# One weight sum in four, of each seven-product gate/up step, made by a negated ScalarE copy and an accumulating DMA

## The reference

```python
def swiglu(h, w_gate, w_up, w_down):
    return (jax.nn.silu(h @ w_gate) * (h @ w_up)) @ w_down

for i in range(DEPTH):                       # DEPTH = 2
    ...                                      # token mixer
    h = rmsnorm(x, g[2])
    x = x + rmsnorm(swiglu(h, ffn_w_gate[i], ffn_w_up[i], ffn_w_down[i]), g[3])
```

## Time and profile before

| | us |
|---|---|
| median of 3 runs | 1317.84 (1317.77 to 1318.12) |
| profiled execution, its own time | 1318.55 |
| its span, first to last instruction | 1316.7 |
| TensorE busy | 1305.5 (99%) |
| VectorE busy | 991.8 (75%) |
| ScalarE busy | 602.3 (46%) |
| GpSimd busy | 68.2 (5%) |

### The profile page before, as it was taken

How to read it: one execution, slowest core, us unless ns; L and a number is a source line. 1 busy time by engine, 2 the same in 40 slices (tenths; PEclk the granted TensorE clock), 3 DMA queues, 4 the chain that set the end, 5 groups by cost and what they waited for, 6 DMA issues and landing times. The chain is left out here.

```text
span 1316.7 us, 19176 instructions
## 1 busy us (share of the span) xinstructions
PE 1305.5 (99%) x7889; PEld 1160.5 (88%) x7889; DVE 991.8 (75%) x1035; ACT 602.3 (46%) x736; POOL 68.2 (5%) x112
## 2 busy tenths in 40 slices
PE   9999999999999999999999999999999999999998
PEld 6878888888889999999888988898898999998886
DVE  6997767789668788887587676577478888884893
ACT  6443444346443444344263455557345344442551
POOL 1000000000010000000000121021010000000000
PEclk9999999999999999999999999999999999999999
DMA  7262514154433333324503132314233233317001
GB/s 236 77 239 63 169 32 160 61 171 170 183 96 117 107 110 86 111 81 147 206 0 112 33 112 72 104 48 160 65 111 113 81 113 97 112 49 272 33 32 64
DMA packets 103413, 145.10 MB, mean 110 GB/s; under 512 B 3580, under 2 KB 77564, under 8 KB 102822
## 3 DMA queue, kind: packets, MB, share of 16 engines
q1 hardware_dynamic: 93168, 136.65, 31.5%
q10 hardware_dynamic: 10166, 7.32, 1.8%
HBM read 137.65 MB, written 8.41 MB: 111 GB/s over the span
## 5 line engine op out<-in xcount | busy, mean ns | idle before, releaser
L2370 PE MATMUL ps<-h_hi,w_hi 128*128 128x256 f32 (+1 forms) x688 | 224.8, 327 | 0.0
L2372 PE MATMUL ps<-h_hi,w_lo 128*128 128x256 f32 (+1 forms) x688 | 223.7, 325 | 0.0
L2371 PE MATMUL ps<-h_lo,w_hi 128*128 128x256 f32 (+1 forms) x688 | 223.6, 325 | 0.0
L1525 DVE TENSOR_TENSOR w_lo<-raw,w_hi 128x2048 fp32r<-128x2048 f32 (+1 forms) x59 | 121.7, 2062 | 72.8 <-ACT w_hi L936 42.9
L2370 PE MATMUL ps<-w_hi,act_hi 128*128 128x512 f32 x432 | 168.7, 391 | 0.1
L2372 PE MATMUL ps<-w_hi,act_lo 128*128 128x512 f32 x432 | 168.2, 389 | 0.0
L2371 PE MATMUL ps<-w_lo,act_hi 128*128 128x512 f32 x432 | 168.1, 389 | 0.0
L2370 PEld LDWEIGHTS ps<-h_hi,w_hi 128*128 128x128 f32 x688 | 130.9, 190 | 11.0 <-issue 0.3
L2372 PEld LDWEIGHTS ps<-h_hi,w_lo 128*128 128x128 f32 x688 | 130.9, 190 | 10.7
L2371 PEld LDWEIGHTS ps<-h_lo,w_hi 128*128 128x128 f32 x688 | 130.9, 190 | 10.3
L1153 ACT ACTIVATE w_hi<-w_sum 128x1024 fp32r<-128x1024 f32 x48 | 50.9, 1061 | 121.7 <-DVE w_sum L1867 121.7
(11 more groups left out here) (328 smaller groups left out, 3232.1 us busy)
## 6 DMA issues: line engine op xcount, KB each, us to landing
raw<-in_ffn_w_down SPq DMA_DIRECT2D x14, 1024.0 KB, 5.4
x<-in_ret_w_in SPq DMA_DIRECT2D x13, 1024.0 KB, 5.2
raw<-in_ffn_w_up SPq DMA_DIRECT2D x24, 512.0 KB, 4.4
raw<-in_ffn_w_gate SPq DMA_DIRECT2D x24, 512.0 KB, 3.9
raw<-in_ret_w_in SPq DMA_DIRECT2D x10, 1024.0 KB, 5.5
down_raw<-in_ffn_w_down SPq DMA_DIRECT2D x8, 1024.0 KB, 9.4
raw<-in_diff_w_in SPq DMA_DIRECT2D x8, 1024.0 KB, 5.3
tmp<-in_ffn_w_gate SPq DMA_DIRECT2D x12, 512.0 KB, 4.0
```

The source lines that it names most:

```text
L1525: nc.vector.tensor_tensor(out_ap, whole, high.bitcast(F32), ALU.subtract).then_inc(done, 1)
L2370: nc.tensor.matmul(out_ap, a_hi, b_hi, start=start, stop=False, skip_group_check=shared)
L2371: nc.tensor.matmul(out_ap, a_hi, b_lo, start=False, stop=False, skip_group_check=shared)
L2372: return nc.tensor.matmul(out_ap, a_lo, b_hi, start=False, stop=stop, skip_group_check=shared)
```

## The change

T3 of steps 3 to 10 is no longer a VectorE subtraction. ScalarE writes minus B12 into T3's place (`t3_negate`, an activation with scale -1), and GpSimd issues two DMAs that read B22 once more from HBM and add it to what stands there (`add_t3`), 256 KB each. Step 2 keeps its VectorE sum. ScalarE's high part of T3 waits for both DMAs (`t3_added`), and moves behind those of B21 and B22; VectorE's low part of T3 moves from the end of step n to the start of step n+1, between `second_hidden` and the low part of B22. The load that overwrites B12's piece waits for the negation instead of the sum.

```diff
-SUMS = Order((n, f) for n in SEVEN for f in ("T1", "T2", "T4", "T3"))
+SUMS = Order([(PLAIN, f) for f in ("T1", "T2", "T4", "T3")] + [(n, f) for n in SEVEN[1:] for f in ("T1", "T2", "T4")])
 HIGHS = Order([(PLAIN, f) for f in ("T4", "B21", "B22", "B11", "T2", "T1", "T3")]
-              + [(n, f) for n in SEVEN[1:] for f in ("B11", "T1", "T2", "T3", "B21", "B22", "T4")])
+              + [(n, f) for n in SEVEN[1:] for f in ("B11", "T1", "T2", "B21", "B22", "T3", "T4")])
...
+def added(l, n):
+    return l * (len(SEVEN) - 1) + n - PLAIN
...
@@ SyncE, load_piece
-                    sp.wait_ge(t_made, SUMS.at(l, m, {"B11": "T1", "B12": "T3", "B22": "T3", "B21": "T4"}[old]))
+                    if m == PLAIN:
+                        sp.wait_ge(t_made, SUMS.at(l, m, {"B11": "T1", "B12": "T3", "B22": "T3", "B21": "T4"}[old]))
+                    else:
+                        sp.wait_ge(t_made, SUMS.at(l, m, {"B11": "T1", "B12": "T1", "B22": "T2", "B21": "T4"}[old]))
+                        if old == "B12":
+                            sp.wait_ge(t3_negated, added(l, m))
@@ GpSimd
+            def add_t3(l):
+                for n in SEVEN[1:]:
+                    pool.wait_ge(t3_negated, added(l, n))
+                    for k in (0, 2):
+                        pool.dma_start(quarter(form_sum(l, n, "T3"))[:, k:k + 2, :],
+                                       up_w[l][:, 4 + k:6 + k, n * 256:(n + 1) * 256], accum_op=ALU.add).then_inc(t3_added, 16)
+
             boundary(0)
+            add_t3(0)
             boundary(1)
...
@@ ScalarE
+                elif f == "T3" and n > PLAIN:
+                    act.wait_ge(t3_added, 32 * added(l, n))
+                    src = form_sum(l, n, f)
...
+            def t3_negate(l, n):
+
+                act.wait_ge(form_used, USED.at(l, n - 1, "T3"))
+                act.wait_ge(piece_sem(n, "B12"), piece_count(l, n, "B12"))
+                nc.scalar.activation(form_sum(l, n, "T3"), piece(l, n, "B12"), ACT.Copy, scale=-1.0).then_inc(t3_negated, 1)
...
+                    if more:
+                        t3_negate(l, n + 1)
                     first_silu(l, n)
                     if more:
-                        for f in ("T3", "B21", "B22"):
+                        for f in ("B21", "B22", "T3"):
                             form_high(l, n + 1, f)
@@ VectorE, gate_up
                         second_hidden(l, n - 1)
+                        form_low(l, n, "T3")
                         form_low(l, n, "B22")
...
                         form_low(l, n + 1, "T1")
-                        weight_sum(l, n + 1, "T3")
                     else:
                         a_low(2 * l + 1, 0, u % 2)
                     make_c12(l, n)
-                    if more:
-                        form_low(l, n + 1, "T3")
                     first_hidden(l, n)
```

More of the change, by code:

```diff
@@ L88 @@
 USED = Order((n, f) for n in SEVEN for f in PRODUCTS)
-SUMS = Order((n, f) for n in SEVEN for f in ("T1", "T2", "T4", "T3"))
+SUMS = Order([(PLAIN, f) for f in ("T1", "T2", "T4", "T3")] + [(n, f) for n in SEVEN[1:] for f in ("T1", "T2", "T4")])
 HIGHS = Order([(PLAIN, f) for f in ("T4", "B21", "B22", "B11", "T2", "T1", "T3")]
-              + [(n, f) for n in SEVEN[1:] for f in ("B11", "T1", "T2", "T3", "B21", "B22", "T4")])
+              + [(n, f) for n in SEVEN[1:] for f in ("B11", "T1", "T2", "B21", "B22", "T3", "T4")])
 LOWS = Order([(PLAIN, f) for f in ("T4", "B21", "B22", "B11", "T2", "T1", "T3")]
-             + [(n, f) for n in SEVEN[1:] for f in ("B11", "T2", "T1", "T3", "B21", "B22", "T4")])
+             + [(n, f) for n in SEVEN[1:] for f in ("B11", "T2", "T1", "B21", "T3", "B22", "T4")])
 S_SUMS = Order((0, f) for f in ("A21", "A22", "A11", "S1", "A12", "S2", "S3", "S4"))
@@ L376, in build @@
         t_made = sem("t_made")
+        t3_negated = sem("t3_negated")
+        t3_added = sem("t3_added")
         form_hi_made = sem("form_hi_made")
@@ L751, in closing @@
                 if c % 2:
-                    sp.wait_ge(t_made, SUMS.at(c // 2, FFN_N - 1, "T3"))
+                    sp.wait_ge(t_made, SUMS.at(c // 2, FFN_N - 1, "T4"))
+                    sp.wait_ge(t3_negated, added(c // 2, FFN_N - 1))
                     sp.wait_ge(form_split, LOWS.at(c // 2, FFN_N - 1, "B11"))
@@ L915, in _ @@
             boundary(2)
+            add_t3(1)
             boundary(3)
```

## The result

| | before | after |
|---|---|---|
| median | 1317.98 us (4 runs) | 1366.84 us (4 runs, 1365.22 to 1367.91) |
| ratio | | 1.0369, interval 1.0351 to 1.0387 |
| span of the profiled execution | 1316.7 | 1363.4 |
| granted clock over the span | 0.998 | 0.989 |

The change costs 48.9 us, 3.7%. The prediction, 1317.8 in a range of 1316 to 1330, was wrong. The busy line of the page, to be held against the earlier trace rows, shows that the work moved: VectorE 22 us less (19 to 20 forecast), ScalarE 10 more (17 forecast; ScalarE instructions that stand back to back overlap by about 0.1 us in these rows, and more of them do now), 32 GpSimd instructions more. TensorE's recorded busy time rose by 13 us with the same number of matmuls.

The account below looks back on a forecast made before the run. The prediction took TensorE as the bound, busy 1305.5 of 1316.7 us. All terms of the change came to 0: 1318.55 + 0 for the profiled execution, 1317.8 on the median, range 1316 to 1330.

Parts of the forecast that it names:

- What bounds the kernel: Seven-product steps: TensorE never waits, 20.16 us a step, so taking 19.5 us off VectorE is worth 0.
- rival 4: Stages behind the steps: a lighter VectorE leaves them earlier, winning at most 5.9 us, so 1312; chance 0.03.
- How long X may be: T3's and VectorE's queue deadlines for TensorE: X up to 11.0 us is free, beyond it 16 (X - 11.0) us.
- X: Time from the negated copy's end until both accumulating DMAs have landed: taken as 7.2 us, 9.2 in series, at most 17.2.
- Rival 1: ScalarE's wait before T3's high part: accumulation lands too late, from X = 11.0 on, 1337 to 1417 us; chance 0.12.
- The prediction's own sign of being wrong: TensorE: first-line matmuls of T3, B22 or T4 wait for VectorE in 16 equal gaps; then X is over 11 us.
- Rival 2: GpSimd's DMA issues: VectorE holds them up, 3.1 us each, X = 11.6, 10 us lost, 1328; chance 0.05.
- rule of the Trainium skill that the prediction weighed: GpSimd's issues: only VectorE's two-port modes block descriptor writing, tensor_tensor lacks them, so no hold-up and the sum stays 0.

Follow-up runs that it names:

- the order test: Kernel before, VectorE still making T3, with only T3's high and low parts at the places the change gives them: 1317.02 us, ratio 0.9993.
- both cures: Changed kernel with the negated copy ahead of T1's and T2's high parts and 2560 bytes per partition for GpSimd's descriptors: 1317.64 us, ratio 1.0000.
- third-DMA run with the copy first: Changed kernel with the negated copy ahead of T1's and T2's high parts and a third 256 KB accumulating DMA per step: 1404.12 us, ratio 1.0650.

## Why the prediction was wrong

**What bounds the kernel: right.** TensorE sets the pace and there was nothing to win. The run without DMAs (0.9999, with VectorE 18 us lighter) and the order test (0.9993) show it; rival 4, a gain from a lighter VectorE, found nothing.

**The step that failed: "How long X may be".** It allowed X 11.0 us. It took the negated copy of the next step as tied to the end of product T3, 1.4 us behind it, and counted the queue behind T3's low part only as far as u4 and c22, where TensorE waits. It counted the two sums between u4 and c22 as time of VectorE, but did not follow the first of them, T2, across to ScalarE: T2's high part waits for it there, and the change put the copy behind that high part. So a late T3 makes the next T3 late with no help from TensorE: the ring is 12.5 us + X. The bound is 20.16 - 12.47 = 7.7 us, not 11.0. The runs on both sides of it agree: X of 5.4 and 6.8 costs nothing or is caught up, X of 11 costs 3.2 us a step, and with the copy moved ahead of the two high parts X of 11.4 is free. Rival 1 named the right place, ScalarE's wait ahead of T3's high part, but with the wrong point and price: at the mean X that came, 10.95, it forecast no loss. The prediction's own sign of being wrong came by half: product T3 does wait for VectorE, in 14 gaps, but X is not over 11 in the mean.

**The second miss: the size of X.** I took 7.2, with 9.2 if the DMAs went in series; it is 10.4 to 12.5 over the 16 steps, 10.95 in the mean. They do go in series, which 1 KB per partition of descriptor room brings about, and each lands 5.0 us after issue begins (median) where I had 4.6 with the issue; of the rest, 0.37 us lie between the copy's end and the first issue in the step shown (498.88 to 499.25). Where both are issued back to back (2048 bytes, 10 steps) X is 6.8 to 9.0, 7.1 in the median, close to the 7.2, but that is luck in part: I had one issue of 0.6 us and 2.6 us more for adding; measured are two issues of 1.2 us each, and an X without hold-up that is 1.7 us longer than the 5.4 of plain copies, 1.0 of which is longer issuing. With that X the changed kernel would have been within 0.2% in spite of the first error, as the run with 2560 bytes is. A figure of the Trainium skill would have misled more: it (DMA: Bandwidth & Descriptors, "Anatomy of one DMA — SWDGE (gpsimd) path") gives 2.0 us + bytes / 436 GB/s, an estimate of 2.6 us for 256 KB; measured here are 4.2 us for a plain copy and 5.0 for an accumulation, counted from the start of the issue, so with 0.72 and 1.21 us of GpSimd's own time in them. The measurement decides.

**Rival 2, that VectorE holds up GpSimd's issues.** GpSimd's 32 issues take 1.20 to 1.38 us each, not 3.1. In the step shown the first issue, at 499.25 for 1.21 us, falls into a VectorE instruction with two SBUF inputs; the second, at 504.99 for 1.22 us, falls almost wholly into VectorE's idle time:

```profile
498.63 2.35 DVE L1558 TENSOR_TENSOR w_lo<-w_sum,w_hi 128x1024 fp32r<-128x1024 f32 x2
...
503.95 1.22 DVE L1558 TENSOR_TENSOR spare_lo<-raw,spare_hi 128x1024 fp32r<-128x1024 f32 x1
511.18 0.69 DVE L1943 TENSOR_TENSOR hidden<-mix 128x512 f32<-128x512 f32 x1 [6.01 <-ACT mix L1215]
```

So VectorE did not stretch them. By the rule of the Trainium skill that the prediction weighed (SBUF — State Buffer, "Who interferes with whom") this was to be expected, and the trace agrees. Something did hold up GpSimd, the room for descriptors, but not VectorE. A fixed cost of using GpSimd for DMAs shows nowhere: with both cures and all 32 of them the time is 1317.64 us against 1317.28.

**The clock.** TensorE's 13 us more of recorded busy time and its 35.0 us of waits for T3's low part make up 48 us, but they are how the loss shows on TensorE, not its cause. Product T3 starts after an idle gap and runs for part of its length at the lower clock (0.52 from 490.06 to 493.50, so 1.2 of 2.4 GHz):

```profile
490.06 0.45 PE L2401 MATMUL ps<-h_hi,w_hi 128*128 128x256 f32 x1 [2.79 <-DVE w_lo L1558]
```

The copy, at 497.84, starts over 3 us after this product's end, so the ring does not go through TensorE and the slowness falls into time that TensorE would have waited. Only in the last step of a layer can it add something: product T3 takes 4.2 us in that of layer 0 (630.72 to 634.90) instead of 2.9, 1.3 us at most. Where the ring does go through it, as in the third-DMA run with the copy first, the same thing costs 2.6 us in the step shown.

## What to carry to other kernels

When an asynchronous step goes into hand-written in-order lists, draw every ring that contains it, not only those that pass the bounding engine: from the waiting instruction along its own list, across each wait to the other engines' lists, until the next round's start of the same step. The slack is the bound's period minus the rest of the longest such ring, and it can be far smaller than the slack of the operand itself (here 7.7 against 11.0 us). Here the cheapest cure was the place in the list: two places on ScalarE were worth 48 us, and nothing of the transfer had to get faster.

## What the runs showed of the hardware

- Two accumulating DMAs of 256 KB issued in a row by GpSimd ran in series with 1024 bytes per partition of descriptor room: the second issue stood for 4.4 to 6.3 us in 16 of 16 steps. With 2048 bytes it did so in 6, with 2560 in 2, at the same two places in two kernels; two plain copies with 1024 bytes in 5 of 16, every third pair.
- GpSimd needs 1.21 us (median) to issue an accumulating DMA of 256 KB and 0.72 for a plain one; SyncE's loads take 0.37 us of its time.
- After 4.35 us of idleness TensorE was granted 0.50 of its clock for the whole of the next product, 5.5 us, and 1.00 behind it (third DMA, copy first). After 2.79 us of idleness in the changed kernel the granted clock was 0.52 (nearly all of it at 1.2 GHz) from 490.06 to 493.50, and the full clock came back behind it.
- The changed kernel's times spread more than those of before: 1365.22 to 1367.91 against 1317.77 to 1318.36 us. The landing of each DMA, 4.3 to 7.2 us after its issue begins, stands in its ring, which is the likely reason; it was not tested:

```profile
DMA to landing us min/median/max: 4.3/5.0/7.2
```
